# Five of sixteen closing tiles go through ScalarE and accumulating transfers

## The chip, the cores and the metric

The kernel runs on one core of one Trainium2 chip. The metric is device time in microseconds for one execution; lower is better. A core has five engines with instruction streams of their own: TensorE (PE, matrix products and transposes), VectorE (DVE), ScalarE (ACT), GpSimd (POOL) and SyncE (SP), which here only issues transfers. Sixteen DMA engines move data between HBM, the chip's memory, and SBUF, the memory that the engines work on. TensorE writes to PSUM, which has eight banks of 128 x 512 words here. Engines wait for each other through semaphores.

## The reference, cut to what matters

One layer of a hybrid encoder on 512 tokens of 2048 channels, all in float32. After the mixer (attention and a recurrence) comes the part at whose end the change lies:

```
x = x + RMSNorm_post(y)                          # y from the mixer; this x is "the residual"
h = rmsnorm(x, norm_ffn_pre)
y = conv_gated_mlp(h, ...)                       # ends with (gelu(g) * up) @ w_down
x = x + rmsnorm(y, norm_ffn_post)                # rmsnorm: y * rsqrt(mean(y*y) + EPS) * gain
```

The last line is what the kernel's last 15 us compute: each token's y times one factor, each channel times its gain, plus the residual.

## The kernel before, in words

Everything but the down projection is held channel-major: a tensor of 2048 channels by 512 tokens is sixteen tiles (`KT = 16`), tile `k` having channels 128k to 128k+127 on its partitions and the 512 tokens along its rows, 2 KB a row and 256 KB a tile. The output `out` in HBM has the same layout, (128, 16, 512).

The residual does not stay in SBUF. When it is made, about 740 to 782 us into the span, ScalarE's queue stores its sixteen tiles to `out` itself (`act.dma_start(out[:, k], x1[:, k])`, L811), which is its parking place. Much later, in the down projection, GpSimd's queue loads all of it back into `x1_b` (L548), which the views call `x_b`, and counts `x1_back_landed`.

The down projection gives y token-major, in four tiles of 128 tokens (`QT = 4`): `y_a` holds two and `y_b` two. At the end VectorE and ScalarE scale each token's row by its root factor (`y_scaled_d`, `y_scaled_a`). Then TensorE turns y back to channel-major: `lift(k, i)` transposes the 128 x 128 block of tile k and token group i into bank `k % 8` (L2053), and `lifted` counts tiles. Tiles 0 to 3 are lifted token group by token group as these are scaled, and the others one after the other. From tile 8 on a bank is used a second time, so that TensorE first waits for `taken` to be k - 7.

VectorE takes the tiles in order (L1667): one instruction multiplies the bank by the channel's gain (`g_ffn_post`), adds the residual's tile `x1_b[:, k]` and writes it back there; `taken` counts. SyncE waits for each count and issues the store of that tile to `out` (L460). At the end it waits until all sixteen have landed (`stored`); that wait has no line of its own and is written L137 in the views.

GpSimd's queue is also used earlier for accumulating transfers: `pool.dma_start(raw_s3[:], weights[...], accum_op=ALU.add)` adds a tile of weights from HBM onto what lies in SBUF, 128 rows of 4 KB (L510 and L515, in the fast product of the feed-forward part, 865 to 1650 us). In the views queue q0 is that of GpSimd and q1 that of SyncE.

Of the kernel before, what the change touches and what calls it, by code (L numbers as in the profile page):

```python
# [25 lines left out]
ALU = mybir.AluOpType  # L26
ACT = mybir.ActivationFunctionType
# [5 lines left out]
KT = D // P  # L33
# [6 lines left out]
QT = S // P  # L40
# [51 lines left out]
OUT_PARTS = (((0, 0, 4, 0),), ((0, 4, 7, 0), (1, 0, 1, 3)), ((1, 1, 5, 0),), ((1, 5, 8, 0), (0, 7, 8, 3)))  # L92
Y_ORDER = (0, 1, 2, 3, 4, 5, 6, 8, 9, 10, 11, 12, 13, 14, 7, 15)
AFTER_Y = 2 * KT
OPEN = 8
LINE = 64
LOG1P = [1.0 / n for n in (15, 13, 11, 9, 7, 5, 3)]
# [7 lines left out]
def at_least(eng, sem, value):  # L105

    if isinstance(value, int) and value <= 0:
        return
    eng.wait_ge(sem, value)
# [23 lines left out]
def block_kernel(nc, xT, par_d, weights, gate_w, out):  # L133
# [3 lines left out]
    with ExitStack() as ctx:  # L137
# [6 lines left out]
        def sem(name):  # L144
# [18 lines left out]
        banks = [ctx.enter_context(nc.psum_tensor(f"bank{i}", [P, S], F32)) for i in range(8)]  # L163
# [98 lines left out]
        x1_b = sb_in(fin, "x1_b", [KT, S])  # L262
# [13 lines left out]
            a11_landed a12_landed a22_landed s3_half s3_landed s2_done s4_done  # L276
            p1_copied pu_done pw_done c22_done c11_taken c12_done c12_taken c21_done last_done
            wd_taken wdsq_done y_summed y_std_done y_r_done y_scaled_a y_scaled_d diag_done spread_done eps_y_done
            x1_back_landed lifted taken
            stored dve_chain""".split()  # L280
        (par_landed, hi_done, split_done, unit_used, consts_set, zeros_set,
         act_hi_done, act_split, sq_done, sq_added, sums_cleared, sum_done, std_done, rms_set,
# [11 lines left out]
         a11_landed, a12_landed, a22_landed, s3_half, s3_landed, s2_done, s4_done,  # L294
         p1_copied, pu_done, pw_done, c22_done, c11_taken, c12_done, c12_taken, c21_done, last_done,
         wd_taken, wdsq_done, y_summed, y_std_done, y_r_done, y_scaled_a, y_scaled_d, diag_done, spread_done,
         eps_y_done, x1_back_landed, lifted, taken,
         stored, dve_chain) = [sem(n) for n in names]
        x_landed = [sem(f"x_landed{c}") for c in range(len(X_CHUNKS))]
        raw_landed = [sem(f"raw_landed{s}") for s in range(2)]  # L300
# [6 lines left out]
        def col(name, i=0):  # L307

            c = COLS[name] + i
            return par[:, c:c + 1] if isinstance(c, int) else par[:, bass.ds(c, 1)]  # L310
# [45 lines left out]
        def _(sp):  # L356
# [57 lines left out]
            whole_units((N_OUT + 4) // 2, N_FF // 2)  # L414
            for m in range(OPEN):

                s, half, c = m % 2, m // 4, m % 4 * 2 * P
                four = weights[U_FF:U_FF + OPEN].rearrange("(i h) p n -> h p i n", h=2)[half][:, :, c:c + 2 * P]
                sp.wait_ge(split_done, N_FF + m - 1)
# [35 lines left out]
                    sp.dma_start(raw[:, s], weights[bass.ds(t * 2 + (U_DOWN + s), 1)].rearrange(  # L455
                        "a p n -> p (a n)")).then_inc(raw_landed[s], 16)

            for k in range(KT):
                sp.wait_ge(taken, k + 1)
                sp.dma_start(out[:, k], x1_b[:, k]).then_inc(stored, 16)  # L460
            sp.wait_ge(stored, 16 * KT)


        @block.gpsimd
        def _(pool):
            pool.dma_start(gw[:], gate_w[0]).then_inc(gw_landed, 16)
            pool.memset(eps[:], EPS)
            pool.memset(ones[:], 1.0).then_inc(consts_set, 1)
            pool.memset(ident[:], 0.0).then_inc(zeros_set, 1)
            pool.memset(mask[:], 0.0).then_inc(zeros_set, 1)  # L470
            pool.memset(xr[:, 0:4], 0.0).then_inc(zeros_set, 1)
            pool.memset(acc[:], 0.0).then_inc(zeros_set, 1)
            pool.memset(acc_b[:], 0.0).then_inc(zeros_set, 1)
            pool.memset(pick[:], 0.0).then_inc(zeros_set, 1)
            pool.wait_ge(zeros_set, 6)
            pool.affine_select(out=ident[:], in_=ident[:], compare_op=ALU.not_equal, fill=1.0, base=0,
                               pattern=[[-1, P]], channel_multiplier=1).then_inc(consts_set, 1)
            for e in range(2):
                pool.affine_select(out=pick[:, e], in_=pick[:, e], compare_op=ALU.not_equal, fill=1.0, base=-e,
                                   pattern=[[0, P]], channel_multiplier=1).then_inc(consts_set, 1)  # L480

            pool.affine_select(out=mask[:], in_=mask[:], compare_op=ALU.is_ge, fill=NEG, base=0,
                               pattern=[[-1, P]], channel_multiplier=1).then_inc(consts_set, 1)

            pool.wait_ge(sum_done, 1)
            pool.memset(acc[:], 0.0).then_inc(sums_cleared, 1)
            pool.memset(acc_b[:], 0.0).then_inc(sums_cleared, 1)

            pool.wait_ge(negc_ready, 1)
            pool.dma_start(negc_d, tt[0:2 * NP]).then_inc(negc_stored, 16)  # L490
            pool.wait_ge(negc_stored, 16)
            with pool.Fori(1, NP) as p:
                pool.wait_ge(gw_split, p)
                pool.dma_start(gw[:], gate_w[bass.ds(p, 1)].rearrange("a p m n -> p (a m) n")).then_inc(gw_landed, 16)
                pool.wait_ge(s_taken, p * 6)
                pool.dma_start(negc[:], negc_d[bass.ds(p * 2, 2)].partition_broadcast(P)).then_inc(negc_landed, 16)

            pool.wait_ge(ynorm_ready, 2)
            pool.wait_ge(act_split, AFTER_Y)
            for k in range(KT):  # L500
                pool.wait_ge(unit_used, N_OUT + k)
                pool.dma_start(x1[:, k], xT[:, k]).then_inc(res_landed, 16)

            def store_h(j):
                pool.wait_ge(h_done, j + 1)
                pool.dma_start(h_d[j], h_out[:, j % 2]).then_inc(h_stored[j % 2], 16)

            def add_to_s1(i):
                pool.wait_ge(s1_half[i % 2], i // 2 * 16 + 16)
                pool.dma_start(raw_s1[:, i % 2], weights[U_FF + 4 * (PLAIN + i) + 3], accum_op=ALU.add).then_inc(  # L510
                    s1_landed[i % 2], 16)

            def add_to_s3(i):
                pool.wait_ge(s3_half, 16 * i + 16)
                pool.dma_start(raw_s3[:], weights[U_FF + 4 * (PLAIN + i)], accum_op=ALU.add).then_inc(s3_landed, 16)  # L515

            for j in range(PLAIN - 2):
                store_h(j)
            add_to_s1(0)
            add_to_s3(0)  # L520
            store_h(PLAIN - 2)
            add_to_s1(1)
            for i in range(NS):
                store_h(PLAIN - 1 + i)
                if i + 1 < NS:
                    add_to_s3(i + 1)
                if i + 2 < NS:
                    add_to_s1(i + 2)

            def load_h(n):  # L530
                for e in range(2):
                    pool.wait_ge(h_stored[e], 16 * n + 16)
                half = PER_GROUP // 2
                at_least(pool, h_hi_done, n - half + 1)
                pool.dma_start(h_t[:, 2 * n:2 * n + 2], h_d[2 * n:2 * n + 2].rearrange("a p s -> p a s")).then_inc(
                    h_landed[n % half], 16)

            pool.wait_ge(unit_used, N_HID - 3)
            for n in range(12):
                load_h(n)  # L540
            store_h(FT - 1)
            pool.wait_ge(unit_used, N_HID)
            for n in range(12, PER_GROUP):
                load_h(n)

            pool.wait_ge(x1_stored, 16 * KT)
            pool.wait_ge(h_split, (GROUPS - 1) * PER_GROUP + KT // 2)
            pool.dma_start(x1_b[:], out).then_inc(x1_back_landed, 16)  # L548


        @block.scalar
        def _(act):
# [265 lines left out]
            x1_tile(1)  # L818
            for m in range(1, OPEN):
                x1_tile(2 * m)  # L820
                x1_tile(2 * m + 1)
                split(N_FF + 1 + m, (1 + m) % 2)
            def gain_x1(k):

                act.wait_ge(act_split, AFTER_Y + k + KT // 2 + 1)
                for n in (k, k + KT // 2):
# [83 lines left out]
            for i in range(NS):  # L910
                j = PLAIN + i
# [33 lines left out]
            for g in range(GROUPS):  # L945
                n = g * PER_GROUP
# [20 lines left out]
            def scale_last(i):  # L967
                act.wait_ge(y_r_done, i + 1)
                act.activation(y_tile(i)[:, 3 * S:], DOWN_BANKS[1][i][:], ACT.Copy, scale=y_r[:, i:i + 1]).then_inc(
                    y_scaled_a, 1)  # L970
# [10 lines left out]
            for i in range(QT):  # L981
# [2 lines left out]
                    scale_last(i - 1)  # L984
                token_root(i)
            scale_last(QT - 1)


        @block.vector
        def _(dve):  # L990
# [587 lines left out]
            for i in range(NS):  # L1578
                j, used = PLAIN + i, N_FAST + 7 * i
# [52 lines left out]
            for g in range(GROUPS):  # L1632
                n = g * PER_GROUP
# [29 lines left out]
                                  ALU.mult).then_inc(y_scaled_d, 1)  # L1663
            dve.wait_ge(x1_back_landed, 16)
            for k in range(KT):
                dve.wait_ge(lifted, k + 1)
                dve.scalar_tensor_tensor(out=x1_b[:, k], in0=banks[k % 8][:], scalar=col("g_ffn_post", k),  # L1667
                                         in1=x1_b[:, k], op0=ALU.mult, op1=ALU.add).then_inc(taken, 1)
# [3 lines left out]
        def _(pe):  # L1672
# [267 lines left out]
            for m in range(OPEN):  # L1940
                pe.wait_ge(split_done, N_FF + m + 1)
                for kt in range(2):
                    k = 2 * m + kt
                    pe.wait_ge(act_split, AFTER_Y + k + 1)
                    for i, bank in enumerate((SB[0], SB[1], PT[0], PT[1])):
# [89 lines left out]
            for g in range(GROUPS):  # L2035
                n, out_banks = g * PER_GROUP, DOWN_BANKS[g % 2]
# [22 lines left out]
            pe.wait_ge(y_scaled_d, QT)  # L2059
            for k in range(4):  # L2060
                lift(k, QT - 1).then_inc(lifted, 1)
            pe.wait_ge(y_scaled_a, QT)
            for k in range(4, KT):
                at_least(pe, taken, k - 7)
                for i in range(QT):
                    last = lift(k, i)
                last.then_inc(lifted, 1)
# [60 lines left out]
```

## Time and profile before

| | |
|---|---|
| median of 3 runs | 2231.21 us (2229.57 to 2232.14) |
| profiled execution, its own time | 2229.45 us |
| its span in the trace | 2227.7 us |
| busy share of the span: TensorE | 98% |
| VectorE | 69% |
| ScalarE | 45% |
| GpSimd | 6% |
| instructions | 34413 |

The span goes from the first instruction's start to the last one's end. "Busy" is a share of the whole span, so that it says nothing of its last microseconds. In the views times are in microseconds from the start of the span. Names of tiles stand as out<-in. "Idle before" is the time for which the engine had nothing to run ahead of an instruction, with what ended it. The share of a DMA queue is the time that its packets took, over sixteen engines and the window; since neighbouring packets overlap a little in the record, a full set of engines can show slightly over 100%.

### The profile page before, as it was taken

What the parts mean: (1) busy time and instruction counts of PE and PEld (TensorE: products, weight loads), DVE (VectorE), ACT (ScalarE), POOL (GpSimd) and SP (SyncE); (2) the same over time, 40 slices, a digit from 0 to 9 for tenths busy, and PEclk for the clock granted to TensorE, in tenths of its full rate; (3) what the DMA queues carried; (4) which work ended last, traced back from release to release, by engine and by line L of the source; (5) the groups of instructions that cost most, each with busy time, mean ns of one, the idle gap of its engine ahead of it and who ended that gap; (6) DMA issues with size and microseconds to landing.
All of it is one profiled execution on the core that took longest, in us unless ns stands there. A gap on an engine that the chain in (4) does not pass through costs nothing.

```text
span 2227.7 us, 34413 instructions
## 1 busy us (share of the span) xinstructions
PE 2182.5 (98%) x13320; PEld 1926.8 (86%) x13320; DVE 1530.0 (69%) x2021; ACT 1002.4 (45%) x1274; POOL 140.5 (6%) x207
## 2 busy tenths in 40 slices
PE   7999999999899899999999999999999999999998
PEld 5788888887688688999999999999998888888876
DVE  7777777777755777888888888888884444444445
ACT  5555555446222454444444444444443343343433
POOL 0000000000100000111111111111102000000000
PEclk9999999999999999999999999999999999999999
DMA  5232223222332436777787787777767332333343
GB/s 171 79 98 81 94 89 97 94 94 76 119 127 94 144 110 176 212 206 211 205 213 204 213 212 208 202 205 204 212 178 292 122 95 95 99 99 94 103 161 113
DMA packets 99853, 328.67 MB, mean 148 GB/s; under 512 B 12944, under 2 KB 20240, under 8 KB 99616
## 3 DMA queue, kind: packets, MB, share of 16 engines
q1 hardware_dynamic: 75200, 240.59, 32.3%
q0 software_dynamic: 22240, 82.36, 16.9%
q10 hardware_dynamic: 2304, 4.20, 0.5%
q8 instruction: 77, 1.26, 0.2%
q14 instruction: 32, 0.26, 0.0%
HBM read 306.09 MB, written 21.00 MB: 147 GB/s over the span
## 4 chain that ended last, share of the span: by engine, by line
PE 91%; DVE 5%; issue 2%; ACT 1%; DMA 1%; POOL 0%; SPq 0%; DVEq 0%; ACTq 0%; POOLq 0%
PE bank L1678 29%; PE bank L1676 29%; PE bank L1677 29%; DVE w_all L996 1%; DMA raw<-weights 1%; PE bank L1735 1%; PE bank L1748 1%; ACT w_all L557 1%; DVE x_b L1667 0%; PE bank L1760 0%; PE bank L1759 0%; DVE act_lo L1011 0%; DMA h_t<-h_spill 0%; DVE xc L1185 0%; PE bank L1706 0%
## 5 line engine op out<-in xcount | busy, mean ns | idle before, releaser
L1676 PE MATMUL bank<-act_hi,w_all 128*128 128x512 f32 (+1 forms) x1760 | 619.6, 352 | 25.6 <-DVE act_lo L1011 14.4
L1678 PE MATMUL bank<-act_hi,w_all 128*128 128x512 f32 (+1 forms) x1760 | 614.5, 349 | 0.0
L1677 PE MATMUL bank<-act_lo,w_all 128*128 128x512 f32 (+1 forms) x1760 | 611.8, 348 | 0.0
L1676 PEld LDWEIGHTS bank<-act_hi,w_all 128*128 128x128 f32 x1760 | 332.0, 189 | 75.4 <-issue 22.3
L1678 PEld LDWEIGHTS bank<-act_hi,w_all 128*128 128x128 f32 x1760 | 331.7, 188 | 46.0
L1677 PEld LDWEIGHTS bank<-act_lo,w_all 128*128 128x128 f32 x1760 | 331.9, 189 | 44.3 <-issue 0.2
L1006 DVE TENSOR_TENSOR w_all<-raw,w_all 128x1024 fp32r<-128x1024 f32 x96 | 117.7, 1226 | 288.3 <-ACT w_all L563 288.3
L1678 PE MATMUL bank<-w_all,act_lo 128*128 128x512 f32 x768 | 302.6, 394 | 0.0
L1676 PE MATMUL bank<-w_all,act_hi 128*128 128x512 f32 x768 | 298.2, 388 | 3.3 <-DVE w_all L1006 1.9
L1677 PE MATMUL bank<-w_all,act_hi 128*128 128x512 f32 x768 | 301.1, 392 | 0.0
L996 DVE TENSOR_TENSOR w_all<-raw,w_all 128x1024 fp32r<-128x1024 f32 x136 | 166.4, 1224 | 161.2 <-ACT w_all L557 159.6
L1676 PE MATMUL bank<-tsum,w_all 128*128 128x256 f32 x896 | 247.3, 276 | 0.0
L1677 PE MATMUL bank<-tsum,w_all 128*128 128x256 f32 x896 | 247.3, 276 | 0.0
L1678 PE MATMUL bank<-tsum,w_all 128*128 128x256 f32 x896 | 247.3, 276 | 0.0
L563 ACT ACTIVATE w_all<-raw 128x1024 fp32r<-128x1024 f32 x96 | 101.7, 1059 | 297.6 <-PE bank L1678 283.3
L557 ACT ACTIVATE w_all<-raw 128x1024 fp32r<-128x1024 f32 x136 | 143.3, 1054 | 177.6 <-PE bank L1678 175.1
L905 ACT ACTIVATE w_all<-raw_s 128x1024 fp32r<-128x1024 f32 x112 | 119.1, 1063 | 153.9 <-PE bank L1678 150.7
L1676 PEld LDWEIGHTS bank<-w_all,act_hi 128*128 128x128 f32 x768 | 144.2, 188 | 36.2 <-DVE w_all L1006 2.1
L1677 PEld LDWEIGHTS bank<-w_all,act_hi 128*128 128x128 f32 x768 | 144.2, 188 | 33.7
L1678 PEld LDWEIGHTS bank<-w_all,act_lo 128*128 128x128 f32 x768 | 144.4, 188 | 28.7
L1543 DVE TENSOR_TENSOR w_all<-raw_s,w_all 128x1024 fp32r<-128x1024 f32 x112 | 137.3, 1226 | 46.2 <-ACT w_all L905 44.9
L1676 PEld LDWEIGHTS bank<-tsum,w_all 128*128 128x128 f32 x896 | 168.2, 188 | 0.0
(264 smaller groups left out, 3658.0 us busy)
## 6 DMA issues: line engine op xcount, KB each, us to landing
raw<-weights SPq DMA_DIRECT2D x310, 512.0 KB, 3.5
raw_s<-weights SPq DMA_DIRECT2D x84, 512.0 KB, 4.7
raw_s<-weights POOLq DMA_DIRECT2D x84, 512.0 KB, 5.7
raw_a<-weights SPq DMA_DIRECT2D x42, 512.0 KB, 5.1
h_spill<-h_out POOLq DMA_DIRECT2D x48, 256.0 KB, 3.6
h_t<-h_spill POOLq DMA_DIRECT2D x24, 512.0 KB, 6.1
x<-xT POOLq DMA_DIRECT2D x16, 256.0 KB, 3.1
out<-x ACTq DMA_DIRECT2D x16, 256.0 KB, 2.2
```

The lines of the kernel that those rows point to most:

```text
L557: act.activation(w_hi[s], raw[:, s], ACT.Copy).then_inc(hi_done, 1)
L563: act.activation(wd_hi[s], raw[:, s], ACT.Copy).then_inc(hi_done, 1)
L905: act.activation(w_slot(q)[0], RAW_OF[n](i), ACT.Copy).then_inc(hi_done, 1)
L996: dve.tensor_tensor(w_lo[s], raw[:, s], word(w_hi[s]), ALU.subtract).then_inc(split_done, 1)
L1006: dve.tensor_tensor(wd_lo[s], raw[:, s], word(wd_hi[s]), ALU.subtract).then_inc(split_done, 1)
L1543: dve.tensor_tensor(lo, RAW_OF[n](i), word(hi), ALU.subtract).then_inc(split_done, 1)
L1676: pe.matmul(dst, ah, bh, start=start, stop=False, skip_group_check=goes_on)
L1677: pe.matmul(dst, ah, bl, start=False, stop=False, skip_group_check=goes_on)
L1678: return pe.matmul(dst, al, bh, start=False, stop=stop, skip_group_check=goes_on)
L1735: last[e] = pe.matmul(dst, q, k, start=t == 0, stop=t == 2)
L1748: last = pe.transpose(dst, sm[:, c:c + P], ident[:])
```

## The change

Tiles 4, 5, 6, 7 and 9 (`ACT_LAST`) leave VectorE. For them ScalarE multiplies the bank by the gain and writes the product to `x1_b[:, k]`, over the residual that was loaded there, and counts `taken_a`. GpSimd then issues an accumulating transfer that adds this tile onto `out[:, k]` in HBM, where the parked residual still lies, and `added` counts. VectorE and SyncE skip these tiles. TensorE waits, before it uses a bank a second time, for the counter of the engine that empties it. The wait for `y_scaled_a` stands at the same place as before. The end of the program waits for both kinds of transfer.

```
+ACT_LAST = (4, 5, 6, 7, 9)
...
-            for k in range(KT):
-                sp.wait_ge(taken, k + 1)
+            for n, k in enumerate(k for k in range(KT) if k not in ACT_LAST):
+                sp.wait_ge(taken, n + 1)
                 sp.dma_start(out[:, k], x1_b[:, k]).then_inc(stored, 16)
-            sp.wait_ge(stored, 16 * KT)
+            sp.wait_ge(stored, 16 * (KT - len(ACT_LAST)))
+            sp.wait_ge(added, 16 * len(ACT_LAST))
...
             pool.dma_start(x1_b[:], out).then_inc(x1_back_landed, 16)
+
+            for n, k in enumerate(ACT_LAST):
+                pool.wait_ge(taken_a, n + 1)
+                pool.dma_start(out[:, k], x1_b[:, k], accum_op=ALU.add).then_inc(added, 16)
...
             scale_last(QT - 1)
+            act.wait_ge(x1_back_landed, 16)
+            for k in ACT_LAST:
+                act.wait_ge(lifted, k + 1)
+                act.activation(x1_b[:, k], banks[k % 8][:], ACT.Copy, scale=col("g_ffn_post", k)).then_inc(taken_a, 1)
...
             dve.wait_ge(x1_back_landed, 16)
             for k in range(KT):
+                if k in ACT_LAST:
+                    continue
                 dve.wait_ge(lifted, k + 1)
...
             for k in range(4, KT):
-                at_least(pe, taken, k - 7)
+                if k >= 8:
+                    by_act = k - 8 in ACT_LAST
+                    n = sum((j in ACT_LAST) == by_act for j in range(k - 7))
+                    pe.wait_ge(taken_a if by_act else taken, n)
+                if k == 4:
+                    pe.wait_ge(y_scaled_a, QT)
```

On VectorE, this stands at the end of the program before, from tile 3 (bank 3) to tile 10 (bank 2). L1667 is the scale-and-add; what an instruction waits for is in brackets:

```order
L1667 SCALAR_TENSOR_TENSOR x1_b<-bank3,par,x1_b 128x512 [waits lifted]
L1667 SCALAR_TENSOR_TENSOR x1_b<-bank4,par,x1_b 128x512 [waits lifted]
L1667 SCALAR_TENSOR_TENSOR x1_b<-bank5,par,x1_b 128x512 [waits lifted]
L1667 SCALAR_TENSOR_TENSOR x1_b<-bank6,par,x1_b 128x512 [waits lifted]
L1667 SCALAR_TENSOR_TENSOR x1_b<-bank7,par,x1_b 128x512 [waits lifted]
L1667 SCALAR_TENSOR_TENSOR x1_b<-bank0,par,x1_b 128x512 [waits lifted]
L1667 SCALAR_TENSOR_TENSOR x1_b<-bank1,par,x1_b 128x512 [waits lifted]
L1667 SCALAR_TENSOR_TENSOR x1_b<-bank2,par,x1_b 128x512 [waits lifted]
```

And of the changed kernel, where the same instruction has L1679, from tile 3 to the last one:

```order
L1679 SCALAR_TENSOR_TENSOR x1_b<-bank3,par,x1_b 128x512 [waits lifted]
L1679 SCALAR_TENSOR_TENSOR x1_b<-bank0,par,x1_b 128x512 [waits lifted]
L1679 SCALAR_TENSOR_TENSOR x1_b<-bank2,par,x1_b 128x512 [waits lifted]
L1679 SCALAR_TENSOR_TENSOR x1_b<-bank3,par,x1_b 128x512 [waits lifted]
L1679 SCALAR_TENSOR_TENSOR x1_b<-bank4,par,x1_b 128x512 [waits lifted]
L1679 SCALAR_TENSOR_TENSOR x1_b<-bank5,par,x1_b 128x512 [waits lifted]
L1679 SCALAR_TENSOR_TENSOR x1_b<-bank6,par,x1_b 128x512 [waits lifted]
L1679 SCALAR_TENSOR_TENSOR x1_b<-bank7,par,x1_b 128x512 [waits lifted]
```

Tile 3 is followed at once by tile 8, and then by 10 to 15.

On ScalarE, the end of the program was the last token scaling into `y_b` from bank 7; in the changed kernel that is followed by the five tiles (L996), whose banks 4 to 7 and 1 are those of tiles 4 to 7 and 9:

```order
L975 ACTIVATE y_b<-bank7,y_r 128x512 [waits y_r_done]
L996 ACTIVATE x1_b<-bank4,par 128x512 [waits lifted,x1_back_landed]
L996 ACTIVATE x1_b<-bank5,par 128x512 [waits lifted]
L996 ACTIVATE x1_b<-bank6,par 128x512 [waits lifted]
L996 ACTIVATE x1_b<-bank7,par 128x512 [waits lifted]
L996 ACTIVATE x1_b<-bank1,par 128x512 [waits lifted]
```

These rows are new, and nothing stands behind them on ScalarE. GpSimd likewise has five issues at L554 behind its load of the residual, and SyncE eleven in place of sixteen.

## Rows read from the trace of the kernel before

**Rows 1.** The page: span, and shares of the chain that ended last
```profile
span 2227.7 us, 34413 instructions
...
PE 91%; DVE 5%; issue 2%; ACT 1%; DMA 1%; POOL 0%; SPq 0%; DVEq 0%; ACTq 0%; POOLq 0%
```

**Rows 2.** Chain in order of time, 2211 to 2228: start us, us, what
```profile
2210.60 0.58 ACT y_b L969
...
2213.12 6.66 DVE x_b L1667 x10
2219.78 0.66 DVEq L137
2220.44 3.29 DVE x_b L1667 x5
```

**Rows 3.** Windows of one microsecond; DMA share is the last but one
```profile
core 0: us, PE busy (x) PEld busy (x) DVE busy (x) ACT busy (x) POOL busy (x), PEclk, DMA share, GB/s
...
2215.00:2216.00 1.00, 1.00 (x12) 1.00 (x11) 1.00 (x3) 0.00 (x0) 0.00 (x0) 1.00 1.06 379
...
2217.00:2218.00 1.00, 1.00 (x8) 0.58 (x7) 1.00 (x3) 0.00 (x0) 0.00 (x0) 1.00 0.50 184
2218.00:2219.00 1.00, 1.00 (x8) 0.69 (x7) 1.00 (x2) 0.00 (x0) 0.00 (x0) 1.00 0.85 313
...
2224.00:2225.00 1.00, 0.00 (x0) 0.00 (x0) 0.00 (x0) 0.00 (x0) 0.00 (x0) 0.50 1.03 387
```

**Rows 4.** DMA view of 2222 to 2224: packets, rate, share of each queue
```profile
DMA packets 421, 0.76 MB, mean 382 GB/s; under 512 B 48, under 2 KB 48, under 8 KB 421
...
q1 hardware_dynamic: 421, 0.76, 102.4%
```

**Rows 5.** Groups by line, 2205 to 2228, and ScalarE's last timeline row
```profile
L1667 DVE SCALAR_TENSOR_TENSOR x_b<-bank,par,x_b 128x512 f32<-128x512 f32 x16 | 10.6, 741 | 0.5 <-PE bank L2053 0.5
...
2211.59 0.69 ACT L969 ACTIVATE y_b<-bank,y_r 128x512 f32<-128x512 f32 x1 [0.23 <-DVE y_r L1660]
```

**Rows 6.** SyncE: issues of L460, min/median/max ns, and its waits
```profile
L460 SPq DMA_DIRECT2D out<-x_b x16: 332/618/1174, 2213.9 to 2224.0; - x16
...
SPq L137 <- DMA out<-x_b: 2.7, 1, 2.7
```

**Rows 7.** TensorE: tiles 4 and 5 begin; its loads from 2205 to 2228
```profile
2213.16 0.38 PE L2053 MATMUL bank<-ident,y_a 128*128 128x128 f32 x2
...
2213.60 0.38 PE L2053 MATMUL bank<-ident,y_a 128*128 128x128 f32 x2
...
L2053 PEld LDWEIGHTS bank<-ident,y_a 128*128 128x128 f32 x32 | 3.8, 140 | 0.8 <-DVE x_b L1667 0.7
```

**Rows 8.** GpSimd: issues of L510, L506 and L548, ns; landing, us
```profile
L510 POOL DMA_DIRECT2D raw_s<-weights x42: 861/872/921, 865.9 to 1642.5; - x42
...
L506 POOL DMA_DIRECT2D h_spill<-h_out x48: 542/578/912, 818.8 to 1692.1; - x48
...
L548 POOL DMA_DIRECT2D x_b<-out x1: 549/549/549, 2113.3 to 2113.3; - x1
...
DMA to landing us min/median/max: 15.4/15.4/15.4
...
1031.38 0.87 POOL L510 DMA_DIRECT2D raw_s<-weights  x1 [8.66 <-DMA raw_s<-weights]
```

**Rows 9.** DMA view, accumulating transfers (q0): 1026 to 1028, then 1031.3 to 1037
```profile
q0 software_dynamic: 80, 0.26, 66.9%
q1 hardware_dynamic: 67, 0.27, 36.7%
...
DMA  5442000000069340929921959899898977700000
...
q0 software_dynamic: 144, 0.52, 56.9%
```

**Rows 10.** DMA view of 1028 to 1030: plain transfers of 4 KB rows
```profile
q1 hardware_dynamic: 206, 0.75, 98.8%
```

More of the change, by code:

```diff
@@ L278, in block_kernel @@
             wd_taken wdsq_done y_summed y_std_done y_r_done y_scaled_a y_scaled_d diag_done spread_done eps_y_done
-            x1_back_landed lifted taken
+            x1_back_landed lifted taken taken_a added
             stored dve_chain""".split()
@@ L296, in block_kernel @@
          wd_taken, wdsq_done, y_summed, y_std_done, y_r_done, y_scaled_a, y_scaled_d, diag_done, spread_done,
-         eps_y_done, x1_back_landed, lifted, taken,
+         eps_y_done, x1_back_landed, lifted, taken, taken_a, added,
          stored, dve_chain) = [sem(n) for n in names]
@@ L2061, in _ @@
                 lift(k, QT - 1).then_inc(lifted, 1)
-            pe.wait_ge(y_scaled_a, QT)
             for k in range(4, KT):
-                at_least(pe, taken, k - 7)
+                if k >= 8:
[4 more added lines that the diff above has]
+                    pe.wait_ge(y_scaled_a, QT)
                 for i in range(QT):
```

## The prediction

> **What bounds the kernel now.** The change touches the last 15 us only, so I read the end. The page says that 91% of the chain is TensorE [rows 1]; all of that lies before the sixteen output tiles and stays. The span is 2227.7 us, the profiled execution's own time 2229.45 us, 1.75 us more, and the median of three runs is 2231.21 us, another 1.76 us more; I work out a difference in the span and add it to the median.
>
> The chain in order of time [rows 2] blames VectorE: from 2213.12 us on it is nothing but L1667, the scale-and-add of the sixteen tiles, and 0.66 us of its own queue between two of them. But it ends at 2223.73 us, 4 us before the span does, because it follows instructions and not transfers. So the next view is the table of one-microsecond windows [rows 3]. The DMA engines, all sixteen together, stand at a share of 1.00 or more in nearly every window from 2215 to 2226. The exceptions are two neighbours, 0.50 and 0.85: 0.65 us of idle time. After 2224 us no engine computes any more, and the DMA engines are still full. Their rate at the end is 382 GB/s [rows 4]. A tile is 128 rows of 2 KB, 0.262 MB, so a plain store takes 0.262 / 382 = 0.69 us of all sixteen engines, and sixteen take 11.0 us. VectorE makes a tile in 10.63 / 16 = 0.66 us [rows 5]. Two resources therefore run at almost the same pace, and the DMA engines are the slower one. SyncE shows it too [rows 6]: its shortest issue takes 0.33 us, the median one 0.62 us, one takes 1.17 us, though each does the same thing; I read the longer ones as an issue that finds its queue full. After the last issue SyncE waits 2.7 us for data to land, and the program ends.
>
> **The change part by part.**
>
> VectorE loses five of sixteen scale-and-adds: 5 x 0.66 = 3.3 us. It would end at about 2220.4 us in place of 2223.73 us. This is the whole of what the change can give, if the transfers follow.
>
> ScalarE gains five scalings from PSUM, 128x512. The nearest row, L969 on the same shape and also scaled by a column, is 0.69 us, and consecutive steps of the chain give it 0.58 us [rows 2, 5]. ScalarE's last instruction ends at 2212.28 us [rows 5], so it is free for them. Their input: TensorE lifts one tile per 0.44 us while nothing holds it (four transposes; tile 4 begins at 2213.16 and tile 5 at 2213.60 us [rows 7]). Tile 4 is lifted at about 2213.75, so ScalarE makes it by 2214.4 and the fifth one, tile 9, by about 2216.6 us. The new wait of ScalarE for the parked residual costs nothing: that load was issued at 2113.3 us and landed after 15.4 us [rows 8]. Behind it only the five scalings are queued.
>
> TensorE's waits for a free bank become two counters. Tiles 12 to 15 wait for ScalarE's tiles 4 to 7, done by about 2216 us, in place of VectorE's, so the three waits of its loads for VectorE, 0.7 us in all, go away [rows 7]. Behind them VectorE's tiles 12 to 15 are queued, which it reaches at 2217.7 us and later; they are ready. Counted from 2213.1 in steps of 0.66, VectorE wants tile 8, its fifth, at 2215.8 us, and counted in steps of 0.44 it is lifted at about 2215.4 us; tile 10 is wanted at 2216.4 and lifted at 2216.3: no wait above 0.1 us.
>
> GpSimd gains five issues. An accumulating issue takes 0.87 us for 512 KB, a plain one 0.58 us for 256 KB [rows 8]; even at 0.9 us five of them, from 2214.5 us on, are done by 2219 us. Nothing else is queued on it. From the issue at 1031.38 us to its first data were 1.5 us (the digits in rows 9 are busy tenths of forty slices of 0.14 us, the first four belong to an older transfer, and it starts in the twelfth), so here the data should start near 2216 us.
>
> The transfers are the term that counts. Eleven plain stores: 11 x 0.69 = 7.6 us. Five accumulating ones, onto rows of 2 KB in HBM: the trace has no such transfer. It has accumulating ones of 4 KB rows onto SBUF. In steady flow they hold 66.9% of the engines for 2 us to move 0.26 MB, exactly one tile: 1.34 us [rows 9]. A whole one of 0.52 MB with its start and end costs 56.9% of 5.7 us = 3.24 us, so 1.62 us a tile [rows 9]. Plain 4 KB rows beside it move 0.75 MB in 98.8% of 2 us, 0.69 us a tile [rows 10], the same per byte as the 2 KB rows of the tail. So for plain transfers halving the row costs nothing, and an accumulate costs 1.9 to 2.3 times the plain one. I take 1.45 us, nearer to steady flow because the queues stay full. The bounds: below, an accumulate onto HBM as cheap as a plain store, 0.69 us; above, 2 KB rows that cost as much each as the 4 KB ones, 2.7 us a tile.
>
> Do the two queues overlap inside an engine, so that the accumulating one is free? In rows 9 the queues' shares are 66.9% and 36.7%, together 103.6%: no more than the tail's plain stores alone show (102%). They add.
>
> The Trainium skill, page "DMA: Bandwidth & Descriptors", section "Issuing engines are not separate DMA queues", says that transfers of ScalarE, SyncE and GpSimd end up on the same sixteen engines and interleave, so that spreading them saves issue time alone. By that rule the five transfers moved to GpSimd bring nothing on the engines; the trace agrees, by the 103.6%. The same page, "Anatomy of one DMA", prices the movement of any transfer at its bytes over 436 GB/s, 0.60 us for a tile, with no surcharge for accumulating; the 1.34 us of rows 9 speak against it for these.
>
> The sum: 7.6 + 5 x 1.45 = 14.8 us of full engines against 11.0 us, +3.8 us. The 0.65 us hole at 2217.5 us is filled, since GpSimd's transfers are queued by then: -0.65 us. The time of the first data and that from the last data to the end stay. +3.15 us: span 2230.9 us, its own time 2232.6 us, median 2231.21 + 3.15 = 2234.4 us. VectorE's 3.3 us are real but bring nothing: the stores behind it are what is late.
>
> **The rivals.** A difference under 0.2%, 4.5 us, is about what a measurement of this kernel can't tell from none.
>
> *The bytes decide* (chance 0.10). An accumulating row costs what a plain one does. For it: TensorE, ScalarE and DMA work as before, 4.2 MB either way, and the skill's price above. Against: rows 9. Then only the hole is won: -0.65 us, 2230.6 us, no change.
>
> *VectorE decides* (0.05). The tail follows VectorE's end, as the chain says, and all 3.3 us come back: 2227.9 us, still within 0.2%. For it: rows 2. Against: DMA windows that are full after 2224 us with VectorE idle [rows 3]. Even this does not reach "faster".
>
> *A row costs the same at 2 KB as at 4 KB when it accumulates* (0.13). Each packet would read its destination from HBM and the price is a latency and not a rate. 7.6 + 5 x 2.68 = 21.0 us against 11.0, less 0.65: +9.3 us, 2240.5 us, slower by 0.4%. For it: no accumulate onto HBM is in the trace, and the start of a 4 KB one costs more than its steady flow (3.24 us against 2.68). Against: plain rows cost by bytes. It decides "slower" from 1.71 us a tile on, (4.46 - 3.15) / 5 = 0.26 us above my value.
>
> **How the numbers follow.** My own case has 0.67, with a range of its own from 1.34 us a tile (+2.6 us) to 1.62 us (+4.0 us), widened by the 1.3 us by which single runs lie from their median: 2232.5 to 2236.5 us. The remaining 0.05 is something unseen. To hold 8 in 10 the range goes down to the rival of the bytes and up into the dear one: 2230.3 to 2239.0 us. Faster by over 0.2% would need more than VectorE can give: 0.02. Slower: the dear rival's 0.13, about a tenth of my case and part of the unseen, 0.24. Within 0.2%: 0.74.
>
> **What the profile will show.** VectorE's last tile ends at 2220 to 2221 us, 11 of them; five L996 scalings of about 0.69 us between 2213.7 and 2217 us. If I am right, the DMA share is full without a hole from 2215 to about 2229.5 us, and the accumulating queue's share times the window is 7 us. If the queue takes 3.5 us, the bytes rival holds; if 13 us, the dear one. If there are idle DMA windows before the end, my sum is wrong as such: then the end is set by a chain of issues and landings, for example GpSimd's last accumulate landing long after the plain stores. That would be the unseen case. The prediction fails most easily at the price of one accumulating tile: each 0.1 us moves the result by 0.5 us.

## The result and the profile after

The changed kernel takes 2235.76 us (median of 20 runs, 2233.84 to 2237.40), and the kernel before, in as many runs, 2231.81 us (2227.49 to 2234.28): a ratio of 1.0019, 95% interval 1.0012 to 1.0025. It is slower by 4 us. The ratio lies within the 0.2% that the prediction called no change, but its interval reaches over that bound. The forecast was +3.15 us. A second set gave a ratio of 1.0012 (1.0003 to 1.0021).

The profiled execution's own time is 2234.11 us. These are the lines of its page that answer to [rows 1]:

```profile
span 2232.4 us, 34415 instructions
...
PE 90%; DVE 5%; issue 2%; ACT 1%; DMA 1%; POOL 0%; SPq 0%; DVEq 0%; ACTq 0%; POOLq 0%
```

The span is 4.7 us longer than in [rows 1], but not all of it belongs to the end. In the timeline of the changed kernel (start, duration, engine and line, count) the closing tiles begin at 2214.59 us, 1.5 us later than in [rows 2]:

```profile
2214.59 7.35 DVE L1679 SCALAR_TENSOR_TENSOR x_b<-bank,par,x_b 128x512 f32<-128x512 f32 x11 [0.50 <-PE bank L2065]
...
2215.34 3.00 ACT L996 ACTIVATE x_b<-bank,par 128x512 f32<-128x512 f32 x5 [1.58 <-PE bank L2065]
...
2216.32 4.44 POOL L554 DMA_DIRECT2D out<-x_b  x5 [99.61 <-ACT x_b L996]
...
2215.37 12.80 SPq L461 DMA_DIRECT2D out<-x_b  x11
```

So I compare **the tail**: from the start of the first of VectorE's scale-and-adds to the end of the span. Before it is 2227.7 - 2213.1 = 14.6 us, after 2232.4 - 2214.6 = 17.8 us: **+3.2 us**. VectorE's eleven tiles take 7.35 us in place of 10.63, ScalarE's five 3.00 us. Both did what was forecast. The windows of one microsecond answer to [rows 3] (the DMA share is the last but one):

```profile
2216.00:2217.00 1.00, 1.00 (x12) 1.00 (x10) 1.00 (x2) 1.00 (x3) 0.68 (x2) 1.00 0.81 293
2217.00:2218.00 1.00, 1.00 (x11) 1.00 (x10) 1.00 (x3) 1.00 (x3) 1.00 (x3) 1.00 1.09 250
2218.00:2219.00 1.00, 1.00 (x11) 1.00 (x10) 1.00 (x2) 0.34 (x1) 1.00 (x4) 1.00 0.80 121
...
2222.00:2223.00 1.00, 0.00 (x0) 0.00 (x0) 0.00 (x0) 0.00 (x0) 0.00 (x0) 1.00 1.13 277
...
2224.00:2225.00 1.00, 0.00 (x0) 0.00 (x0) 0.00 (x0) 0.00 (x0) 0.00 (x0) 1.00 1.11 252
...
2229.00:2230.00 1.00, 0.00 (x0) 0.00 (x0) 0.00 (x0) 0.00 (x0) 0.00 (x0) 0.50 1.04 402
2230.00:2231.00 1.00, 0.00 (x0) 0.00 (x0) 0.00 (x0) 0.00 (x0) 0.00 (x0) 0.50 1.01 387
2231.00:2232.40 1.40, 0.00 (x0) 0.00 (x0) 0.00 (x0) 0.00 (x0) 0.00 (x0) 0.50 0.11 40
```

VectorE ends at 2221.94 us. The DMA engines go on for 9 us more, always full. From 2219 to 2228, while both queues are served, the share is 1.07 to 1.13; from 2229 on plain stores alone are left (1.04, 402 GB/s). The hole of [rows 3] has shrunk to 0.20 us, at 2218. Queue by queue over the whole tail, against one queue at 102.4% in [rows 4]:

```profile
q0 software_dynamic: 720, 1.31, 44.3%
q1 hardware_dynamic: 1584, 2.88, 44.2%
q8 instruction: 1, 0.02, 0.4%
```

The accumulating queue took 44.3% of 17.8 us, 7.9 us of all sixteen engines, so 1.58 us a tile; q1 took 7.9 us for eleven stores, 0.72 us each. A third queue, q8, moved one packet of 0.02 MB, a fetch of instructions; it matters below. And the issues, which answer to [rows 6, 8] (min/median/max ns):

```profile
L461 SPq DMA_DIRECT2D out<-x_b x11: 343/1202/1712, 2215.4 to 2227.0; - x11
...
L554 POOL DMA_DIRECT2D out<-x_b x5: 909/1532/2133, 2216.3 to 2218.6; - x5
...
DMA to landing us min/median/max: 4.6/7.9/10.6
```

SyncE's median issue went from 0.62 to 1.20 us: its queue is emptied more slowly. GpSimd's issues overlap and grow from 0.91 to 2.13 us.

### The profile page after: what moved, and what is told of

Same layout as the page of the kernel before. It is cut to its first block, busy times and chain, and to the rows that moved or that the text cites. A ratio compares the mean times of both kernels' runs of the same rounds, so it can differ in the third digit from the quotient of the medians.

```text
span 2232.4 us, 34415 instructions
## 1 busy us (share of the span) xinstructions
PE 2185.5 (98%) x13320; PEld 1929.4 (86%) x13320; DVE 1526.8 (68%) x2016; ACT 1005.4 (45%) x1279; POOL 145.0 (6%) x212
## 4 chain that ended last, share of the span: by engine, by line
PE 90%; DVE 5%; issue 2%; ACT 1%; DMA 1%; POOL 0%; SPq 0%; DVEq 0%; ACTq 0%; POOLq 0%
PE bank L1688 29%; PE bank L1689 29%; PE bank L1690 29%; DMA raw<-weights 1%; PE bank L1747 1%; DVE w_all L1006 1%; PE bank L1760 1%; ACT w_all L563 1%; PE bank L1772 0%; PE bank L1771 0%; DVE x_b L1679 0%; DVE act_lo L1021 0%; DVE xc L1195 0%; PE bank L1718 0%; DVE act_lo L1342 0%
## 5 line engine op out<-in xcount | busy, mean ns | idle before, releaser
L1688 PEld LDWEIGHTS bank<-act_hi,w_all 128*128 128x128 f32 x1760 | 332.4, 189 | 76.2 <-issue 22.2
```

Source lines behind the costliest of these rows:

```text
L1688: pe.matmul(dst, ah, bh, start=start, stop=False, skip_group_check=goes_on)
```

## The experiments

The tail is the main reading, since it leaves out what happens in the 2213 us ahead of it. Every trace of these runs gives one value, and two traces of one kernel differ by 0.2 us (before) and 0.6 us (changed), so a difference of a few tenths says nothing; the whole time is given where it was measured in several rounds.

| kernel | tail, us | VectorE's tiles, us |
|---|---|---|
| before, and again | 14.6, 14.8 | 10.63 |
| changed, and again | 17.8, 18.4 | 7.35 |
| five plain, from GpSimd | 14.7 | 7.35 |
| five scaled by ScalarE, all stored by SyncE | 14.8 | 7.35 |
| two accumulated | 16.6 | 9.31 |
| ten accumulated | 24.0 | (two pieces) |
| the last five accumulated | 20.9 | 7.33 |
| five accumulated, all made by VectorE | 19.0 | 10.62 |
| five accumulated, rows of 4 KB | 18.5 | 7.36 |
| before, two issuing queues | 14.5 | 10.63 |
| before, half rows | 12.7 | 10.63 |
| split, half rows | 11.3 | 7.36 |

**The changed kernel again.** No edit.

> The changed kernel itself, for a second trace. The tail is counted from the start of VectorE's first scale-and-add to the end of the span; it was 14.6 us before and 17.8 us in the changed kernel, while the tiles began 1.5 us later in the span of the changed one. Theory A, the extra time is made in the tail by the DMA engines: the tail is again 17.5 to 18.1 us, and the start of the tiles can lie anywhere within some 3 us of the first trace. Rival, the change also delays what is ahead of the tail: the tiles again begin 1.5 us or more later than in the kernel before. Against the kernel before 3 to 4 us slower.

Measured: 2234.96 us against 2231.61 us, ratio 1.0012 (1.0003 to 1.0021). Tail 2233.1 - 2214.72 = 18.4 us, a little above what was expected. The tiles began at 2214.72 us. The kernel before, traced again (below), began them at 2216.91 us, later than either trace of the changed one; so where the tail begins moves by up to 3.8 us between executions of one kernel, and the 1.5 us are not the change's.

**Five plain stores from GpSimd.** The residual is left out of these five tiles.

```
-                pool.dma_start(out[:, k], x1_b[:, k], accum_op=ALU.add).then_inc(added, 16)
+                pool.dma_start(out[:, k], x1_b[:, k]).then_inc(added, 16)
```

> The five transfers of GpSimd are plain stores in place of accumulating ones, so the residual is left out of five tiles; all else as changed. Theory A, an accumulate costs twice the engine time of a store: the tail falls by 5 x (1.42 to 1.58 - 0.70) = 3.6 to 4.4 us, to 13.4 to 14.2 us, about as the kernel before less its hole. Rival, issuing from GpSimd or the two counters cost the time: the tail stays above 16.5 us. Rival, VectorE decides: 14.6 - 3.3 = 11.3 us.

Measured: 2232.00 us against 2231.61 us, ratio 0.9998 (0.9989 to 1.0007); tail 14.7 us. The DMA view of its tail and GpSimd's issues:

```profile
q1 hardware_dynamic: 1584, 2.88, 52.8%
q0 software_dynamic: 400, 1.31, 24.5%
...
L554 POOL DMA_DIRECT2D out<-x_b x5: 540/540/560, 2218.3 to 2220.6; - x5
```

With the accumulate gone, 3.1 to 3.7 us of tail are gone, and the new waits, the second queue and ScalarE's part cost nothing. GpSimd's queue falls to 24.5% of 14.7 us, 0.72 us a tile, and its issues to 0.54 us each. The tail misses the expectation from above, though: its 13.4 to 14.2 us took the hole to be won, and what was measured is the tail of the kernel before, 14.6 to 14.8 us.

**SyncE stores all sixteen**, five of them again without the residual. GpSimd's part goes, and SyncE waits for the maker of each tile:

```
+            for k in range(KT):
+                by_act = k in ACT_LAST
+                n = sum((j in ACT_LAST) == by_act for j in range(k + 1))
+                sp.wait_ge(taken_a if by_act else taken, n)
+                sp.dma_start(out[:, k], x1_b[:, k]).then_inc(stored, 16)
```

> ScalarE scales the five tiles as in the changed kernel, but SyncE stores all sixteen plainly and in order of the tiles; the residual is left out of five tiles. It shows what 3.3 us of VectorE are worth by themselves. Theory A, the DMA engines pace the tail: the tail is 14.0 to 14.6 us, that of the kernel before, though VectorE ends about 3 us sooner. Rival, VectorE decides: 11.3 us, and 3.3 us faster than the kernel before.

Measured: 2232.91 us, ratio 1.0004 (0.9995 to 1.0013); tail 14.8 us, just above the 14.0 to 14.6 us expected and far from VectorE's 11.3. In its timeline and its list of issues VectorE is done after 7.35 us, and the stores still go out to the old pace:

```profile
2217.74 7.35 DVE L1677 SCALAR_TENSOR_TENSOR x_b<-bank,par,x_b 128x512 f32<-128x512 f32 x11 [0.50 <-PE bank L2063]
...
L463 SPq DMA_DIRECT2D out<-x_b x16: 343/634/1667, 2218.5 to 2229.1; - x16
...
DMA to landing us min/median/max: 2.5/3.2/3.9
```

3.3 us less of VectorE on the path that the chain names are worth nothing here.

**Two and ten tiles accumulated.**

```
-ACT_LAST = (4, 5, 6, 7, 9)
+ACT_LAST = (4, 5, 6, 7, 8, 9, 10, 11, 12, 13)
```

and `(5, 7)` for the other.

> Ten tiles in place of five (4 to 13) go through ScalarE and accumulating transfers. Theory A, each adds 0.72 to 0.88 us of engine time and the hole is won once: the tail is 17.8 + 5 x 0.72 to 0.88 = 21.4 to 22.2 us, 7 us and more above the kernel before (about 0.3% slower). Rival, the 3.2 us are a fixed price of one more queue (its start, its last landing): the tail stays at 17.5 to 18.5 us.

> Two tiles (5 and 7) in place of five go through ScalarE and accumulating transfers. Theory A, the engines' time per tile, 0.64 to 0.73 us more than a store as the changed kernel less the plain stores of GpSimd gave, and no fixed part: the tail is 14.65 + 2 x 0.64 to 0.73 = 15.9 to 16.2 us. Rival, most of the 3.2 us is fixed: 17.5 us or more.

Measured: ten give 2242.03 us, ratio 1.0047 (1.0032 to 1.0063), and a tail of 24.0 us; two give 16.6 us. Both lie above what was expected (21.4 to 22.2 us, 15.9 to 16.2 us), and each is nearer to that than to its rival (17.5 to 18.5 us, 17.5 us or more). The tail grows with the number: 14.7 us for none (the plain stores from GpSimd), 16.6 for two, 18.1 for five (mean of two traces), 24.0 for ten. No fixed price of a second queue explains that, but it is not a straight line either. Two cost 0.95 us each, five 0.68 us. At two the DMA engines do not finish together; its last windows:

```profile
2230.00:2231.00 1.00, 0.00 (x0) 0.00 (x0) 0.00 (x0) 0.00 (x0) 0.00 (x0) 0.50 0.99 381
2231.00:2232.00 1.00, 0.00 (x0) 0.00 (x0) 0.00 (x0) 0.00 (x0) 0.00 (x0) 0.50 0.14 53
2232.00:2233.00 1.00, 0.00 (x0) 0.00 (x0) 0.00 (x0) 0.00 (x0) 0.00 (x0) 0.50 0.04 16
```

For the last microsecond and more one or two engines of sixteen work, so this tail holds more than the price of two accumulates. The last windows of the ten and its issues show where the upper end leaves the line:

```profile
2233.00:2234.00 1.00, 0.00 (x0) 0.00 (x0) 0.00 (x0) 0.00 (x0) 0.00 (x0) 0.50 1.12 203
2234.00:2235.00 1.00, 0.00 (x0) 0.00 (x0) 0.00 (x0) 0.00 (x0) 0.00 (x0) 0.50 0.57 102
2235.00:2236.00 1.00, 0.00 (x0) 0.00 (x0) 0.00 (x0) 0.00 (x0) 0.00 (x0) 0.50 0.04 6
2236.00:2238.60 2.60, 0.00 (x0) 0.00 (x0) 0.00 (x0) 0.00 (x0) 0.00 (x0) 0.50 0.00 0
...
L554 POOL DMA_DIRECT2D out<-x_b x10: 907/2282/3660, 2216.4 to 2221.5; - x10
```

The data end near 2235.5 us, and the span goes on until 2238.6: 3 us with nothing in the DMA engines. The next run shows what fills them. Without the 2.3 us that this is longer than in the other kernels, ten cost (24.0 - 2.3 - 14.7) / 10 = 0.70 us each.

**The last five accumulated.** `ACT_LAST = (11, 12, 13, 14, 15)`.

> The five tiles are the last ones, 11 to 15, in place of 4, 5, 6, 7 and 9. With ten tiles the accumulating transfers were last, and 3.0 us passed from the last data to the end of the span, against 0.7 us where a plain store was last. Theory C, the landing of an accumulate comes 2.3 us later after its data than that of a store, and the choice of early tiles hides that: the data end at 16.5 to 17.7 us as in the changed kernel, and the tail is 19.5 to 20.7 us. Rival, the 3.0 us are the backlog of ten of GpSimd's transfers: the tail is 17.5 to 18.5 us.

Measured: tail 20.9 us. Its last windows:

```profile
2231.00:2232.00 1.00, 0.00 (x0) 0.00 (x0) 0.00 (x0) 0.00 (x0) 0.00 (x0) 0.50 1.09 256
2232.00:2233.00 1.00, 0.00 (x0) 0.00 (x0) 0.00 (x0) 0.00 (x0) 0.00 (x0) 0.50 0.55 172
2233.00:2235.60 2.60, 0.00 (x0) 0.00 (x0) 0.00 (x0) 0.00 (x0) 0.00 (x0) 0.50 0.00 0
```

The data end near 2233.0 us and 2.6 us of nothing follow. So the rival, a backlog of ten (17.5 to 18.5 us), fell. But theory C is wrong in its cause too, though its tail (19.5 to 20.7 us) is only 0.2 us off: no accumulate lands late. In the trace all counts of landed transfers have arrived by 2233.34 us, 0.3 to 0.4 us after the last data of their queue, and SyncE is through its waits at 2233.39 us. What the program then waits for is a DRAIN that stands at the end of GpSimd's stream (start as given, duration in ns; in the kernel with plain stores from GpSimd below it):

```profile
L138 POOLq DRAIN  x1: 13551/13551/13551, 2221.8 to 2221.8; - x1
L138 SPq COMPARE_BRANCH  x1: 38/38/38, 2233.4 to 2233.4; - x1
L138 SPq EVENT_SEMAPHORE  x1: 17/17/17, 2235.5 to 2235.5; - x1
...
L138 POOLq DRAIN  x1: 8146/8146/8146, 2220.6 to 2220.6; - x1
```

It ends at 2235.37 us, 2.7 us after the last data of GpSimd's queue (2232.68 us), and with ten tiles at 2238.33, 2.8 us after them. In all eight traces with late transfers from GpSimd this distance is 2.6 to 2.8 us, and with plain stores from GpSimd it is 2.7 us (2228.77 after 2226.04), so it belongs to GpSimd's queue and not to the accumulate. That the changed kernel takes early tiles hides it: there the DRAIN ends at 2231.49 us, 0.6 us before SyncE has seen the last store land.

**All tiles by VectorE, five of them accumulated.** The transfers' part alone:

```
+            for k in (4, 5, 6, 7, 9):
+                pool.wait_ge(taken, k + 1)
+                pool.dma_start(out[:, k], x1_b[:, k], accum_op=ALU.add).then_inc(added, 16)
```

> The kernel before, with VectorE on all sixteen tiles and ScalarE on none, but tiles 4, 5, 6, 7 and 9 leave by GpSimd's accumulating transfers (the residual is then in them twice). The transfers' part of the change alone. Theory A, only the transfers count: the tail is 17.3 to 18.6 us, that of the changed kernel, though VectorE ends 3.3 us later than there. Rival, VectorE's relief gives something back that the changed kernel already has in it: up to 3.3 us longer, 21 us.

Measured: tail 19.0 us, above the 17.3 to 18.6 us expected, so neither theory alone. The price is there without ScalarE and without the relief of VectorE. The tail is also 0.6 to 1.2 us longer than that of the changed kernel, as if VectorE's relief gave something back there by way of earlier accumulates; but this is one trace, and the two of the changed kernel are 0.6 us apart. Two windows show a difference; tiles begin at 2215.01 us:

```profile
2218.00:2219.00 1.00, 1.00 (x11) 0.92 (x9) 1.00 (x3) 0.00 (x0) 0.31 (x1) 1.00 0.06 12
2219.00:2220.00 1.00, 1.00 (x8) 0.66 (x7) 1.00 (x3) 0.00 (x0) 1.00 (x2) 1.00 0.71 260
```

Here GpSimd's first accumulate is issued 3.7 us into the tail in place of 1.7, and all engines but one stand empty for 1.2 us; in the changed kernel its data fill that time. That this hole makes the tail longer is not shown: with plain stores a hole of 1.1 us went with 0.2 us of tail (below).

**Rows of 4 KB.** Tiles 4 and 5 are one accumulating transfer, 6 and 7 another, and 9 stays alone:

```
+            for n, k0, k1 in ((2, 4, 6), (4, 6, 8), (5, 9, 10)):
+                pool.wait_ge(taken_a, n)
+                pool.dma_start(out[:, k0:k1].rearrange("p a s -> p (a s)"),
+                               x1_b[:, k0:k1].rearrange("p a s -> p (a s)"), accum_op=ALU.add).then_inc(added, 16)
```

> Tiles 4 and 5 leave in one accumulating transfer of rows of 4 KB, 6 and 7 in another, 9 alone as before: 24 accumulating rows an engine in place of 40, with the same bytes. Theory A, an accumulate is priced by its bytes: the queue's share of the engines' time stays at 7.5 to 8.1 us and the tail at 17.4 to 18.5 us. Rival, by its rows: the queue's time falls to 24/40 of it, 4.8 us, and the tail to about 15 us.

Measured: tail 18.5 us.

```profile
q1 hardware_dynamic: 1584, 2.88, 43.1%
q0 software_dynamic: 432, 1.31, 41.8%
```

432 packets in place of 720, and 41.8% of 18.5 us, 7.7 us of engine time in place of 7.9: between rows of 2 and 4 KB an accumulate is priced by its bytes.

**The kernel before, its stores on two queues**, and **the kernel before again**.

```
+            for k in range(1, KT, 2):
+                act.wait_ge(taken, k + 1)
+                act.dma_start(out[:, k], x1_b[:, k]).then_inc(stored, 16)
```

> The kernel before, with the odd tiles' stores issued from ScalarE's queue and the even ones from SyncE's. In the kernel before one issue of SyncE took 1.17 us and the DMA engines stood empty for 0.65 us behind it. Theory A, that is a limit of one queue: the hole goes away and the tail is 13.8 to 14.1 us in place of 14.6 us. Rival, the hole is something in the engines or in memory: it stays, 14.6 us. In the whole time no difference that can be measured.

> The kernel before, for a second trace of its tail. The first had 14.60 us from the first scale-and-add to the end, with 0.65 us of hole, and the run with two queues, whose hole was 0.4 us, still had 14.51 us. New theory B: the hole never counted, since one DMA engine is held by a fetch of instructions of 16 KB (about 1 us) at the start of the tail, works through the hole and is the last one at the end; the tail is again 14.5 to 14.8 us whatever the hole. Old step: the tail is shorter by as much as the hole is smaller.

Measured: two queues give 2233.05 against 2232.55 us, ratio 1.0001 (0.9992 to 1.0010), and a tail of 14.5 us. The kernel before again has 14.8 us, with a hole of 1.1 us:

```profile
2220.00:2221.00 1.00, 1.00 (x10) 0.81 (x8) 1.00 (x3) 0.00 (x0) 0.00 (x0) 1.00 0.05 10
2221.00:2222.00 1.00, 1.00 (x8) 0.76 (x8) 1.00 (x2) 0.00 (x0) 0.00 (x0) 1.00 0.85 313
```

So a hole of 0.4, 0.65 and 1.1 us goes with tails of 14.5, 14.6 and 14.8 us. The hole is hardly in the sum. The DMA view of the kernel before says why, with its digits (slices of 0.01 us): from 2217.6 us, in the hole; from 2226.55 us, at the very end; then the third queue from 2215 to 2216 us:

```profile
DMA  0500000005000000050000000500000000500000
...
q1 hardware_dynamic: 6, 0.01, 6.7%
...
DMA  0050000000500000005000000050000000500000
...
q1 hardware_dynamic: 6, 0.01, 6.7%
...
q8 instruction: 1, 0.02, 6.0%
```

6.7% of sixteen engines is one engine. One and only one still has rows to move while the others wait in the hole, and one is the last at the end, 0.4 us after the next. Whatever the hole gave to fifteen engines, the sixteenth was never in it. The record doesn't number the engines, but the single packets of the trace tell which one is late. In the kernel before again the fetch of instructions (16 KB, queue q8) lasts from 2218.65 to 2220.30 us. These are two views of its hole, from 2220.00 to 2220.28 and from 2220.28 to 2221.28 us (slices of 0.025 us):

```profile
q1 hardware_dynamic: 2, 0.00, 0.4%
...
DMA  5000000005000000040000002002002002086489
```

Up to 2220.28 us only two packets of 4 bytes start on q1. The next row of 2 KB starts at 2220.289 us, 14 ns before the fetch ends, and seven more follow it end to end. With SyncE's sixteen plain stores it is the same, 3 ns before the end of the fetch. So the late engine is the one that fetched; the rows queued on it waited. From there it works almost without a pause, 0.65 us a tile: in four of the five traces with full plain stores the last data come 10.5 to 10.7 us after the end of the fetch, whatever the hole, and in the fifth, the first trace of the kernel before, where this engine had tile 0 behind it, 10.0 us. In the kernel before again the sixteenth engine ends only 0.04 us after the next, so that a longer hole would have begun to count.

The hole goes with the same fetch. The issue that takes long is under way when the fetch ends, and it ends 0.35 to 0.40 us after it in ten traces, changed kernel included, and 0.53 to 0.73 us after it in three. Which way one holds up the other no run here shows.

**Half rows, without and with the split.** `out[:, k, 0:HS]` from `x1_b[:, k, 0:HS]` in the kernel before, and in the one where SyncE stores all sixteen.

> The kernel before, with the stores of the output cut to the first half of each row, so half of the output is left out. It takes the DMA engines off the tail. Theory A, then VectorE decides: the tail is its 10.6 us and about 3 us for the last store, 13.3 to 13.9 us.

> Plain stores of all sixteen tiles from SyncE with five tiles scaled by ScalarE (no residual in those), and again only the first half of each row stored. With the DMA engines off the tail VectorE's relief must show. Theory A: the tail is VectorE's 7.3 us and about 3 us, 10 to 11.3 us, so 2.5 to 3.3 us below the half rows without the split, where with full rows the same split gave next to nothing. Rival, SyncE's issues pace it: at 0.33 to 0.62 us an issue up to 0.62 x 16 = 9.9 us and 3 us, 13 us, no gain from the split.

Half of the output is left out here. Measured: 0.9988 (0.9978 to 0.9997) and 0.9982 (0.9973 to 0.9991) of the time before; tails 12.7 and 11.3 us.

```profile
L460 SPq DMA_DIRECT2D out<-x_b x16: 332/358/1545, 2218.7 to 2228.6; - x16
...
L463 SPq DMA_DIRECT2D out<-x_b x16: 332/447/952, 2215.1 to 2223.4; - x16
...
2222.00:2223.00 1.00, 0.00 (x0) 0.00 (x0) 0.00 (x0) 0.00 (x0) 0.00 (x0) 1.00 0.80 263
```

Without the split VectorE decides, and the tail is its 10.6 us and 2.1 us more, where 3 us were expected. With the split it falls by 1.4 us, where full rows gave nothing, but not by 3.3 us: VectorE is done after 7.4 us and the engines, at 0.80, are not full. SyncE's sixteen issues take 8.82 us with 0.45 us as their median, and from the long one on they stand back to back. So the pace of the issues is the likely next bound, about 2 us behind the first; that it is SyncE, and not the queue that it fills, is not shown.

## Why the prediction was right

The mechanism was right: the accumulating transfers cost engine time on the resource that bounds. One step failed, and the number came close partly by luck.

**What bounds.** Right: the DMA engines, not the VectorE that the chain names. The same split of the tiles with plain stores moves nothing (14.7 and 14.8 us), while it moves 1.4 us once the stores are halved. With plain stores it is one of the sixteen that ends last. As forecast, the first data (1.6 us into the tail) and the time from the last data to the end (0.7 us) stay.

**VectorE and ScalarE.** Right to 0.1 us: 7.35 us against 7.3, 3.00 us for five scalings; in the closing tiles TensorE waited for no bank.

**GpSimd.** The issues end 4.4 us after the first, as bounded, and data start 3.2 us into the tail against 2.9 forecast.

**The price of an accumulate, 1.45 us.** 1.58 us of engine time, under the 1.62 us of the upper row and above my value; the queue took 7.9 us in place of 7. But "they add" was wrong by a little: while both queues are served, the shares sum to 1.07 to 1.13 and not to 1.03, so that engine time is not quite time. What the tail pays is 0.68 us over a store (five against none), where the sum had 1.45 - 0.69 = 0.76 us: 3.4 us in place of 3.8.

**"The 0.65 us hole at 2217.5 us is filled: -0.65 us."** This step failed. The hole is filled, down to 0.20 us, and nothing comes of it, since one engine is late anyway: five plain stores from GpSimd fill it too, and the tail is 14.7 us. An average over sixteen engines hid the one that decides, and the issue of 1.17 us, read as one that finds its queue full, was under way when that engine's fetch of instructions ended. Without this term the sum is +3.8 us, against +3.4 us by the traces (18.1 - 14.7). The two errors, -0.65 and +0.4 us, partly cancel, and that is luck.

**The sum.** +3.15 us forecast, +3.4 us by the tails, and +4.0 us with an interval of +2.7 to +5.6 us by the medians. With the measured prices (1.58 less 0.70 us) the same additive sum gives +4.4 us less the hole. The dear rival (2.68 us a tile) fell: rows of 2 KB took 1.58 us of engines a tile, and rows of 4 KB the same by the byte. The rival of the bytes fell by the 3.1 to 3.7 us between accumulating and plain stores, VectorE's by the split with plain stores. The unseen case, GpSimd's last accumulate landing long after the plain stores, does not exist as such, but one close to it does: GpSimd's DRAIN, 2.6 to 2.8 us behind its queue's last data. The choice of tiles hid it, which is luck too: with the last five the tail is 20.9 us, 2.8 us longer.

No kernel tried that computes the whole output beats the one before.

## What to carry to other kernels

When a chain of waits ends some microseconds before the span does, look at the DMA share of those last microseconds: an engine that makes 256 KB in 0.66 us ahead of stores that take 0.69 us is not the bound, and taking a third of its work away gave nothing. An accumulating transfer is not a free add: count about twice the engine time of a store, and issue it early: where GpSimd's queue still moved data in the last 0.3 us of the transfers, its DRAIN ended the program about 2 us later than a store of SyncE's does. Before a hole in an averaged DMA share is counted as a gain, look whether all engines are in it: here a fetch of 16 KB of instructions held up one of them for 1 to 1.7 us, and with plain stores that one set the end.

## What the runs showed of the hardware

- Accumulating 256 KB onto HBM took 1.58 us of all sixteen engines, with rows of 2 KB (5 transfers, 7.9 us) and nearly the same with four of the five tiles in rows of 4 KB (7.7 us); a plain store 0.70 to 0.72 us.
- From the last data to the end of the span: about 0.7 us where a store of SyncE's or ScalarE's queue was last by more than 2 us, 2.6 us (the last five) and 3.0 us (ten) where GpSimd's was last or 0.3 us ahead. There GpSimd's closing DRAIN ends the program, 2.6 to 2.8 us after the last data of its queue, accumulating or plain; the counts of landed transfers arrive 0.3 to 0.5 us after the data in either case.
- GpSimd's issue of an accumulate onto HBM took 0.91 us and of a plain store 0.54 to 0.56 us. The accumulating ones, issued 0.57 us apart, grew by 0.3 us each, to 3.66 us for the tenth; the plain ones stayed at 0.54 us. The generating of each seems to take about 0.9 us, one after the other.
- GpSimd's plain stores of tiles with 2 KB rows went out in 400 packets, its accumulating ones in 720: five times 64 against five times 128, and sixteen more for each transfer.
- In every trace one fetch of 16 KB of instructions fell into the tail and took 0.96 to 1.8 us. In the two traces where it can be followed packet by packet the rows queued on its DMA engine waited, and that engine was the last to finish.
- In thirteen of the fourteen traces an issue of SyncE (with two issuing queues one of ScalarE) was under way when this fetch ended and took 0.87 to 1.8 us; with stores from SyncE or ScalarE alone a hole in the transfers came with it. Whether the fetch causes it is open.
